# Constant multiplications on TensorE during its waits for norms, routing and turned attention outputs

## What is computed

```python
def rmsnorm(x, g):
    y = xf * lax.rsqrt(jnp.mean(xf * xf, axis=-1, keepdims=True) + EPS)
    return y.astype(x.dtype) * g

# each layer: a norm, a mixer, a norm, an expert layer or an MLP
h = modulate(rmsnorm(x, ffn_norm_g[layer]), sh2, sc2)
x = x + g2[:, None, :] * grouped_moe(h, router_w, router_bias, ...)
...
x = x + m
x = x + _squared_relu_mlp(_rmsnorm(x, norm2[i]), w_up[i], w_down[i])
```

## Time and profile before

| | |
|---|---|
| median of three runs | 3014.1 us (3011.36 to 3027.58) |
| the profiled execution | 2997.93 us, its span 2996.1 us |
| TensorE busy | 2559.8 us of the span, 85% |
| mean granted TensorE clock | 0.926 of full |
| the same in 40 slices, tenths | 9978799879877879999899999999999899998999 |

### The profile page before, as it was taken

The page is one execution under the profiler, slowest core; times in us unless marked ns, Lnnn a source line. Parts: engine busy times, 40 slices in busy tenths (PEclk is TensorE's granted clock), DMA queues, the critical chain, the costliest instruction groups (busy, mean ns, idle before and its releaser), DMA issues.

```text
span 2996.1 us, 31497 instructions
## 1 busy us (share of the span) xinstructions
PE 2559.8 (85%) x13386; PEld 2192.3 (73%) x13386; DVE 1687.9 (56%) x1448; ACT 1257.4 (42%) x1289; POOL 105.5 (4%) x121
## 2 busy tenths in 40 slices
PE   2867899778656788999798999979998699898999
PEld 2756777567545677778696899768987599886898
DVE  4664777756445477775464455555456545553544
ACT  1334566423233456654333344444444344343443
POOL 1020000000000000000000000000001000000000
PEclk9978799879877879999899999999999899998999
DMA  7840699966253059985354455514544155462453
GB/s 253 234 145 12 218 329 315 331 211 222 76 176 125 5 206 321 325 297 191 104 188 144 155 197 182 169 57 157 196 167 155 43 176 186 152 197 99 164 195 133
DMA packets 262892, 539.78 MB, mean 180 GB/s; under 512 B 12736, under 2 KB 101344, under 8 KB 262752
## 3 DMA queue, kind: packets, MB, share of 16 engines
q1 hardware_dynamic: 242128, 470.91, 46.2%
q0 software_dynamic: 15520, 59.77, 5.7%
q10 hardware_dynamic: 5104, 7.08, 1.2%
HBM read 533.53 MB, written 4.19 MB: 179 GB/s over the span
## 4 chain that ended last, share of the span: by engine, by line
PE 58%; DVE 17%; DMA 12%; ACT 8%; issue 3%; POOL 1%; SPq 1%; ACTq 0%; DVEq 0%; POOLq 0%
DVE w_low L1762 6%; PE Y L914 5%; PE Y L916 5%; PE pair L834 5%; PE pair L835 5%; PE pair L839 5%; PE Y L924 5%; ACT w_high L1397 5%; DMA raw<-in_exp_w_down 4%; PE pair L856 3%; DMA raw<-in_exp_w_gate 3%; DVE work L1787 3%; PE pair L857 3%; PE pair L862 3%; DMA work<-in_w_mod 2%
## 5 line engine op out<-in xcount | busy, mean ns | idle before, releaser
L1762 DVE TENSOR_TENSOR w_low<-raw,w_high 128x2048 fp32r<-128x2048 f32 (+3 forms) x456 | 1022.8, 2247 | 776.9 <-ACT w_high L1397 775.6
L1397 ACT ACTIVATE w_high<-raw 128x2048 fp32r<-128x2048 f32 (+3 forms) x456 | 857.4, 1881 | 1004.9 <-PE Y L924 255.7
L834 PE MATMUL pair<-hT_high,w_high 128*128 128x256 f32 x1280 | 320.6, 287 | 22.9 <-DVE hT_low L1814 22.9
L835 PE MATMUL pair<-hT_low,w_high 128*128 128x256 f32 x1280 | 319.9, 287 | 0.0
L856 PE MATMUL pair<-w_high,hT_high 128*128 128x512 f32 (+2 forms) x644 | 260.1, 405 | 29.5 <-DVE hT_low L1814 13.2
L834 PEld LDWEIGHTS pair<-hT_high,w_high 128*128 128x128 f32 x1280 | 250.3, 196 | 25.5 <-DVE hT_low L1814 24.6
L857 PE MATMUL pair<-w_high,hT_low 128*128 128x512 f32 (+2 forms) x644 | 257.6, 401 | 0.0
L835 PEld LDWEIGHTS pair<-hT_low,w_high 128*128 128x128 f32 x1280 | 250.5, 196 | 0.9
L916 PE MATMUL Y<-w_high,gated_low 128*128 128x512 f32 x528 | 205.8, 390 | 0.0
L914 PE MATMUL Y<-w_high,gated_high 128*128 128x512 f32 x528 | 205.7, 390 | 0.0
L839 PE MATMUL pair<-hT_high,w_low 128*128 128x256 f32 x1280 | 182.4, 286 | 0.0
(11 more groups left out here) (326 smaller groups left out, 3734.7 us busy)
## 6 DMA issues: line engine op xcount, KB each, us to landing
raw<-in_exp_w_gate SPq DMA_DIRECT2D x64, 1024.0 KB, 5.3
raw<-in_exp_w_up SPq DMA_DIRECT2D x64, 1024.0 KB, 5.3
raw<-in_exp_w_down SPq DMA_DIRECT2D x64, 1024.0 KB, 5.0
raw<-in_w_up SPq DMA_DIRECT2D x64, 1024.0 KB, 5.5
raw<-in_w_down SPq DMA_DIRECT2D x64, 1024.0 KB, 5.0
work<-in_w_mod POOLq DMA_DIRECT2D x48, 1024.0 KB, 6.4
raw<-in_ret_w_in SPq DMA_DIRECT2D x48, 1024.0 KB, 5.2
raw<-in_ret_w_out SPq DMA_DIRECT2D x16, 1024.0 KB, 4.9
```

The costliest lines, as they stand in the source:

```text
L834: nc.tensor.matmul(ps[:, f, :], high[:, k, cols_], hT_high[:, k, :], start=(k == 0), stop=False)
L835: nc.tensor.matmul(ps[:, f, :], high[:, k, cols_], hT_low[:, k, :], start=False, stop=False)
L1397: nc.scalar.activation(w_high[:, s % HIGH, 0:n], raw[:, s % RAW, 0:n], ACT.Copy).then_inc(high_ready, 1)
L1762: V.tensor_tensor(w_low[:, s % HIGH, 0:n], part, w_high[:, s % HIGH, 0:n].bitcast(F32), ALU.subtract).then_inc(low_ready, 1)
```

## The change

A helper `keep_busy(n)` issues n multiplications of the fp32 identity by 512 columns of the fp32 masks into the first bank of Y. Their result is never read. It is called with fixed counts: 8 ahead of an ordinary norm's transposes (behind a new wait of TensorE for the update of x) and 8 behind them, 6 behind the transposes of a late norm, 8 behind those of b_norm, 4 before and 4 after the transposes of each attention output, 6 after the router product and 8 after place_tokens, 3 between the transposes of a retention's output, 6 after kv_down and 6 after the modulations behind dq. The first norm of the kernel has none.

```diff
+            def keep_busy(n):
+
+                for _ in range(n):
+                    nc.tensor.matmul(Y[:, 0:512], ident, masks[:], start=True, stop=True)
+
             def norm(n):
+                if n.after and not n.late and not n.again:
+                    pe.wait_ge(updated, TB * n.after)
+                    keep_busy(8)
+
                 def waits(b):
...
                 transposes(n.uses[1], x if n.late else xn, 4)
+                if n.after:
+                    keep_busy(6 if n.late else 8)
                 wait_emptied(pe, n.uses[1])
...
                     weigh(n)
+                keep_busy(4)
                 o_wait()
                 for j in range(2):
                     transposes(a.oT[j], tokpair(o), 4 * j)
+                keep_busy(4)
                 wait_emptied(pe, a.oT[1])
...
                 norm(m.norm)
                 thin_product(m.router, 1)
+                keep_busy(6)
                 place_tokens(m)
+                keep_busy(8)
                 gather_tokens(m)
...
                     transposes(r.oT[j], r_o, 4 * j)
+                    if j == 1:
+                        keep_busy(3)
...
             token_product(plan.kv_down, KD, KV_RANK + ROPE)
+            keep_busy(6)
             pe.wait_ge(latent_ready, 1)
...
                 modulation(mod_use)
+            keep_busy(6)
             pe.wait_ge(latent_ready, 2)
```

## The result

The change makes the kernel slower: 3042.5 us in the median (3029.3 to 3049.0) against 3012.9 us for the kernel before, run beside it (3003.6 to 3027.9). The ratio is 1.0086, with a 95% interval from 1.0064 to 1.0107: 26 us, between 19 and 32. The forecast was 3041.0 us, slower, with a range from 3020 to 3075 us. Time and sign came out as forecast; one step of the working was wrong, several terms were too large, and the errors in part cancelled.

The account below looks back on a forecast made before the run. TensorE was taken to bound the kernel, 85% busy, with 443 us of the span at the low clock. Overruns of 71.9 us less 45 us given back made 27 us, added to 3014.1: 3041 us, range 3020 to 3075.

Parts of the forecast that it names:

- A constant is two passes of 0.43 us: Price of one keep_busy multiplication, from 16 instructions for 8 similar calls: 0.86 us at full clock, 1.7 us at low.
- Overrun = batch less room, ahead of the norms: Five norms: 6.9 us batches in 3.3 us of room, plus 3.9 us for cold starts, 22.1 us too long in sum.
- Behind the transposes: After six norms' transposes: 6.9 us batches in 4.17 or 3.35 us pauses, less faster transposes; net cost 9.1 us.
- Late norms: Six late norms: 5.2 us batches in pauses of about 4.0 us, 1.15 us each, 6.9 us; 9 us given back.
- In the expert layers the router gains nothing: The 48 router multiplications take 10.0 us at 0.50 and 10.2 us at 1.00, so a higher clock saves nothing there.
- the routing's sum: Two expert layers: batches after router and place_tokens 2.15 and 3.0 us too long, 10.3 us, less 2 us for place_tokens.
- Attention and retention outputs: Attention output batches cost 14.1 us and 11 us come back; retention outputs cost 5.0 us and 5 us come back.
- cq: 6 constants after the modulations behind dq, before a 2.6 us pause and at first cold: 4.4 us too long.
- The give-back as a whole: Work behind the batches runs at a higher clock, saving 45 us in all against 71.9 us of overruns.
- The clock that does not come back: Rival: transposes and small products behind batches let the clock fall again, so overruns stand without savings; 3086 us, chance 0.17.
- Hidden time: Rival: slack in expert or modulation weight loads absorbs the delay in expert layers and around dq; 3024 us, chance 0.15.
- The faster cases: Rival: a constant is one pass, 2968 us, or the clock gives back twice as much, 2996 us; chance 0.08.

Follow-up runs that it names:

- the fitted kernel: The change with most counts cut so that each batch ends inside its pause, such as 3 ahead of the norms instead of 8: 2977.4 us, ratio 0.9898.
- further pauses: The fitted kernel plus batches in pauses the change left alone (modulations, waits for x, a retention's last head): 2954.1 us, ratio 0.9809.
- version with three ahead: The change with 3 constants instead of 8 ahead of the five norms, all else as in the change: 3019.2 us, ratio 1.0018.
- the router's kernel: The fitted kernel plus two constants inside each expert layer's 48 router multiplications, after 18 and after 33: 2980.1 us, ratio 0.9883.

## Why the prediction was right, and where it was not

- **A constant is two passes of 0.43 us**: right. 404 instructions, a batch's pairs 0.86 us apart; the factor two against a single pass decides the sign, as the kernel with half the columns shows from the other side (-1.1%).
- **Overrun = batch less room, ahead of the norms**: right, 22.4 and 21.1 for 22.1. The first retention's norm starts cold (+5.7 and +6.0 for 3.6 + 2.3). At the key-value norm the step is +3.76, the same as at a norm that starts warm, where I had added 1.6 us for a cold start. In the first execution the first expert layer's batch had such a cold start instead (+5.3), so that its close agreement is in part luck.
- **Behind the transposes**: mechanism right, net 7.0 and 5.6 in place of 9.1. An ordinary norm has +0.40 in place of 0.9, a retention +1.2 in place of 1.7. b_norm, +3.3 and +1.9, holds 3.0.
- **Late norms**: 0.54 in place of 1.15 us. I took 5.2 us for the batch against 4.0 us of room; from the batch's first start to the product's are 1736.18 - 1731.43 = 4.75 us, and with a step of 0.54 the room was 4.2 us. The product's first multiplication takes 0.68 us there and 0.39 us in the fitted kernel, so its second one is 0.84 us late; counted from that one the give-back is 1.49 us, for the 1.5 us that I had. The net, -3.8 against -2.1 us, was better than forecast.
- **"In the expert layers the router gains nothing"**: wrong. This was the step that failed. I read two stretches of 48 multiplications, 10.0 us at 0.50 and 10.2 us at 1.00, as a pace that does not depend on the clock. The second row is the kernel's first product of this form, not a router. It lies in the first 81 us of the trace, before its first record of the clock, and there 1.00 is not a measurement. In the second profile of the kernel before the same product has the same pace, 0.214 us, and its clock is on record from 62.9 to 79.9 us: 0.50. In the changed kernel the router runs 0.111 us apart while at 1.00, and its 48 take 7.5 us in the first expert layer and 7.1 us in the second in place of 10.05 us, so they gain 2.6 and 2.9 us where I had nothing. That the routing's sum was only 2 us off is luck: the clock that has fallen in mid-router makes the 6 constants behind it too long by 5.1 and 3.7 us, where I had 2.15. The signpost "from the router to the gather about 23.8 us" became 21.8 us (1070.17 to 1091.99), while the one in front of it, 15.8 us, came out at 15.2 us. A second stretch at 1.00 from elsewhere in the trace would have exposed it.
- **Attention and retention outputs**: in the second attention ahead +2.6 for 2.7, behind -1.17 and in the product -1.28; in the third ahead +4.6, behind -0.9, in the product +0.3; in the differential layer +0.00 ahead, +0.4 to +1.0 behind, where I gave 3.0, and -2.2 in the product. In the first retention the third transposes come 3.5 us late and then 2.1 us are given back; in the second the net is between -0.6 and +0.3 us.
- **cq**: +4.3 and +5.1 for 4.4; the uq product behind its transposes gave back some 0.8 us in the first execution and nothing in the second.
- **The give-back as a whole**: about two thirds of the overruns (in the first execution the steps at the batches add up to some 73 us later, what lies behind them to some 50 us earlier), so that the sign is that of the overruns, as forecast. Mean clock 0.944 and 0.950 for 0.955.
- **From span to median**: I added 27 us to the median of the runs shown. The two medians differ by 29.7 us, the ratio's centre says 26 and the places say 22.6, or some 25.7 with the two attentions charged whole. That the total came within 2 us of 3041 owes something to luck: the routing's two errors cancel, and the interval of the comparison alone is 13 us wide.
- **Rivals**. The clock that does not come back is excluded by the fitted counts and by the stretches at 1.00 behind the batches; the product at 1.00 that I held against it was the row misread above. Hidden time is excluded by the doubled constants. The faster cases fail on their conditions: a constant is two passes, and the give-back stays under the 72 us from which it would decide. What turns the idea into a gain is that the overruns go: with counts that fit it is 1.0%, and with further pauses 1.9%.

## What to carry to other kernels

A filler ahead of dependent work costs what it outlasts its pause by, and is worth its place only if the clock gives back more: take the pause from the trace and the filler's length at both clock levels from the nearest rows, and leave a small remainder, since 1.5 us of idle time left over still started the router warm and an excess was paid for nearly in full. The remainder is not quite free: with it the clock fell after 22 router multiplications instead of 32. Size each pause by itself; the same 3 constants cost nothing ahead of the second expert layer's norm and 2.5 us ahead of cq. To judge an edit of a few microseconds where executions scatter by 25, align the same instructions of two traces and read the steps at the edited places.

## What the hardware showed that I had not expected

**The clock falls within unbroken work of narrow multiplications.** The router's 48, with 16 columns, start at 1.00 and go on without a gap, and in their middle the clock goes to 0.50: in the change after 29 and 32 of them in the two expert layers (28 and 33 in its second execution), in the fitted kernel, where the router starts behind a short pause, after 21 and 18. Two constants among them did not prevent it.

**One attention may stay at the low clock for tens of microseconds in one execution and not in the next.** The third attention's inner part in the kernel before and after, where the second window ends with the 5.4 us of the batch ahead of the output; the narrower window below it is that part of the changed kernel which lies wholly at the low level:

```profile
1971.00:2005.90 34.90, 26.35 (x208) 22.63 (x208) 19.87 (x33) 20.81 (x72) 0.00 (x0) 0.93 0.03 9
```
```profile
2003.00:2058.60 55.60, 49.03 (x216) 40.37 (x217) 20.77 (x33) 21.15 (x72) 0.00 (x0) 0.54 0.03 9
2013.00:2057.00 44.00, 41.09 (x176) 34.39 (x176) 14.44 (x26) 16.45 (x53) 0.00 (x0) 0.50 0.00 1
```

And a window over the same attention in the second execution of the change:

```profile
2003.00:2042.00 39.00, 32.68 (x203) 25.72 (x200) 15.85 (x28) 20.35 (x64) 0.00 (x0) 0.82 0.00 1
```

By the ledger the inner part is 15.2 us longer in the change, the larger part of the 28.1 us of the untouched stretches, and 2.1 us in its second execution. Constants are not needed for such a stretch: in the kernel with the wait alone it is the first attention that stays low:

```profile
211.00:265.00 54.00, 45.17 (x248) 38.73 (x246) 21.82 (x34) 25.54 (x77) 0.00 (x0) 0.65 0.00 1
```

beside about the same stretch in the first and in the second profile of the kernel before:

```profile
211.00:251.00 40.00, 29.88 (x253) 25.47 (x251) 21.28 (x32) 25.28 (x77) 0.00 (x0) 1.00 0.00 1
```
```profile
211.00:252.00 41.00, 32.43 (x209) 27.26 (x208) 20.97 (x32) 23.23 (x74) 0.00 (x0) 0.77 0.00 1
```

The step of the ledger across the inner part, against the first profile of the kernel before and without the batch ahead of the output, is 15.2 us in the third attention of the change and of its version with three ahead; in the first attention it is 13.6 us with the wait alone, 13.7 us in the router's kernel, and 7.6 us with transposes as filler and in the second profile of the kernel before. The expert stretches add steps of up to 8 us in the same way. Whether constants make such a stretch likelier is not settled: the 15.2 us in the third attention stand in two of the three profiles of the change and its version with three ahead, and in none of the three without constants. Steps of this size fit the 24 us by which the timed executions of the kernel before differ among themselves; that it is their cause was not shown, since timed executions have no trace. What sets it off is open.

**Transposes of fp32 data count for the clock**, as the kernel filled with them shows: 0.109 us each, a mean clock of 0.949, and a stretch behind a late norm at 1.00.
